# Two adaptive modulations computed with their output columns on the partitions

## The chip, the cores and the metric

The kernel runs on one core of one Trainium2 chip. The metric is the device time of one execution in microseconds. A profile shows one execution: its span, and what TensorE (PE, with its weight loads PEld), VectorE (DVE), ScalarE (ACT), GpSimd (POOL) and SyncE (SP) did in it. Everything is computed in fp32, so TensorE runs two passes for each matmul of the program, and the profile counts both.

## What is computed

Two transformer blocks work one behind the other on x, 512 positions of width 1024. Each starts with a modulation vector of 6 x 1024 numbers, from a condition vector c of its own:

```
mod = silu(c) @ ada_w + ada_b              # c: 1024, ada_w: 1024 x 6144
shift1, scale1, gate1, shift2, scale2, gate2 = split(mod, 6)
h = rmsnorm(x, norm1_w) * (1 + scale1) + shift1
proj = h @ w_in
...                                        # block 1: causal convolution of 4 taps over q, k and v, gated delta
                                           # rule, sparse attention; block 2: pooling and convolution branches
x = x + gate1 * (mixed @ w_out)
h2 = rmsnorm(x, norm2_w) * (1 + scale2) + shift2
...                                        # block 1: feed-forward of width 2816; block 2: retrieved experts
```

## The kernel before

**Layout.** Activations lie with the channels on the 128 partitions: `xT` and `hT` hold 8 channel tiles of 512 positions. The modulation is wanted in the same form: `mod[p, blk, t]` is output 128 t + p of block `blk`, so 48 columns per block, and `eff` is (1 + scale) * norm weight.

**The ada products before.** `ada_w` (25 MB per block) streams on POOL's queue through a ring of four slots, 48 transfers of 512 KB per block, the next into a slot once VectorE has used it (`ada_used`, `ada_2_used`). Inputs lie on the partitions. `matvec` multiplies a tile of 128 inputs x 512 outputs by 128 values of silu(c), one per partition, and adds the next seven tiles to it: 12 groups `g` per block, each one tensor_scalar and seven scalar_tensor_tensor of 512 elements. The sum over the 128 partitions is then made by TensorE: `columns` takes 128 x 128 of the result as weights and a column of ones as the moving operand, which leaves four columns of `mod` in PSUM. `modulation` adds the bias.

**Order of the first block.** The order of each engine is written out by hand; semaphores tie them. VectorE does groups 0 to 2, the first norm, group 3, `modulation(0, 0, 16)`, groups 4 to 7, then `gate_logits`, and with each of the 12 convolutions `conv(m)` half a group of 8 to 11. SP loads param, x and const, and after 8 slots of ada the row weights, the first four w_in tiles and mats. TensorE makes the norm's sum, four groups of columns, the row projection (64 matmuls of 276 columns, result `PS[:, c]`), then 24 w_in blocks `m` of 512 columns, with columns behind blocks 2, 3, 5, 7 and 9, a one-row sum of squares (`many_sum`) behind blocks 2 to 9, the gate's sums behind 3 and the heads' norms (`spread`) from block 11 on, which wait for VectorE's reciprocal (`inverse_many`, behind conv 10). ScalarE applies `eff` and shift to all 8 tiles of `hT`, exponentials of the gate, and Silu and Square of each convolution's result. `conv(m)` on VectorE is one product from PSUM and three multiply-adds (the four taps).

**Second block.** Its ada stream starts after the attention. VectorE does 44 of the 96 half-slot steps beside the 11 double steps of the feed-forward's "up" loop and 52 beside the 8 "down" blocks. TensorE's columns stand behind the first down block (groups 0 to 3), behind the sum of norm 2 (4 to 7) and behind the 28 projections of the second block (8 to 11), ahead of `branches`, which wait for VectorE's layer norm (`yc_ready`). From some 1040 us on, experts are gathered row by row, and `row_dot` (line 2267) multiplies each with the activation and reduces in one tensor_tensor_reduce over 1024 elements, the form that the change uses.

Of the kernel before, what the change touches and what calls it, by code (L numbers as in the profile page):

```python
# [18 lines left out]
P = 128  # L19
S = 512  # L20
# [29 lines left out]
def _cols(widths):  # L50
    out, at = {}, 0
    for name, w in widths:
# [5 lines left out]
    ("ident", P), ("ones", P), ("upper", P), ("strict", P), ("causal", P), ("levels", LEVELS * P),  # L58
    ("cmpneg", NC * NCMP), ("cmpmask", NC * NCMP), ("poolcnt", 4 * 16), ("iota", 16), ("strip", 2 * MANY - 1), ("hscale", 1), ("eps", 1), ("one", 1)])
PARAM, NPARAM = _cols([  # L60
    ("c", KT), ("c_2", KT), ("ada_b", 48), ("ada_b_2", 48), ("norm1", KT), ("norm2", KT), ("norm1_2", KT),
# [6 lines left out]
          ("down", 16, WIDE)]  # L68
FIRST = {}
# [103 lines left out]
def build(nc, a, out):  # L173
    ctx = ExitStack()
    with ctx:
# [15 lines left out]
        silc = sb("silc", [P, 2, KT])  # L191
# [26 lines left out]
        acc = area(19008, 12, S)  # L218
        ring_a = area(26944, SLOTS, 2 * S)
# [52 lines left out]
        acc_2 = area(FT * S + 3072, 12, S)  # L272
        ring_2 = area(FT * S + 9216, SLOTS, 2 * S)
# [140 lines left out]
        modcol_done = sem("modcol_done")  # L414
# [65 lines left out]

        def evicted(t):
# [70 lines left out]
        def _(pe):  # L552
# [32 lines left out]
            def columns(src, blk, g):  # L585

                for q in range(4):
                    ins = mm(PS[:, 6, 48 * blk + 4 * g + q:48 * blk + 4 * g + q + 1], src[:, g, q * P:(q + 1) * P], ones[:, 0:1])
                ins.then_inc(modcol_done, 1)

            pe.wait_ge(inputs_loaded, 32)
            norm(0)

            for g in range(4):
                pe.wait_ge(ada_used, SLOTS * (g + 1))
                columns(acc, 0, g)
            pe.wait_ge(rows_loaded, 16)

            for c in range(NC):
                for k in range(KT):  # L600
                    if c == 0:
                        pe.wait_ge(h_ready, k + 1)
# [41 lines left out]
            def turn(i):  # L644

                if i == 0:
                    pe.wait_ge(mod_ready, 2)
                elif i == 1:
                    pe.wait_ge(hm_normed, 8)
                else:  # L650
                    pe.wait_ge(kv_done, i - 1)
# [6 lines left out]
            for m in range(24):  # L658
# [10 lines left out]
                if m == 2:  # L669
                    for g in range(4, 8):  # L670
                        pe.wait_ge(ada_used, SLOTS * (g + 1))
                        columns(acc, 0, g)
                if m in (3, 5, 7, 9):
                    g = 8 + (m - 3) // 2
                    pe.wait_ge(ada_used, SLOTS * (g + 1))
                    columns(acc, 0, g)
# [128 lines left out]
            pe.wait_ge(rest_loaded, 16)  # L805
# [55 lines left out]
            for m in range(KT):  # L861
                if m == 1:

                    pe.wait_ge(ada_2_used, 4 * SLOTS)
                    for g in range(4):
                        columns(acc_2, 1, g)
# [10 lines left out]
            pe.wait_ge(ada_2_used, 8 * SLOTS)  # L877
            pe.wait_ge(mod_ready, 3)
            for g in range(4, 8):
                columns(acc_2, 1, g)  # L880
# [171 lines left out]
            pe.wait_ge(ada_2_used, 12 * SLOTS)  # L1052
            for g in range(8, 12):
                columns(acc_2, 1, g)
# [82 lines left out]
        def _(act):  # L1137
# [5 lines left out]
            A(silc[:, 0, :], par("c", 0, KT), ACT.Silu).then_inc(silu_c_ready, 1)  # L1143
            act.wait_ge(silu_c_ready, n(silu_c_ready))
            A(silc[:, 1, :], par("c_2", 0, KT), ACT.Silu).then_inc(silu_c_ready, 1)
            act.wait_ge(silu_c_ready, n(silu_c_ready))
            def norm(z, col, shift, final=None, base=0, w=S, parts=None, done=0):
# [14 lines left out]
                for q, part in enumerate([hT] if parts is None else parts):  # L1162
                    for k in range(KT):
                        act.wait_ge(normed, KT * (done + q) + k + 1)
# [30 lines left out]

            for m in range(12):
                act.wait_ge(conv_ready, m + 1)
# [87 lines left out]
            for t in range(NC * NH):  # L1285
# [296 lines left out]
        def _(dve):  # L1582
# [30 lines left out]
            def modulation(blk, lo, hi):  # L1613

                dve.wait_ge(modcol_done, 12 * blk + hi // 4)
                tt(mod[:, blk, lo:hi], PS[:, 6, 48 * blk + lo:48 * blk + hi], par("ada_b" if blk == 0 else "ada_b_2", lo, hi - lo), ADD).then_inc(vec_step, 1)
# [6 lines left out]
            def matvec(blk, g, weights, landed, used, dst, k0=0, k1=KT):  # L1623

                for k in range(k0, k1):
                    j, u = divmod(k, 2)
                    if u == 0:

                        dve.wait_ge(landed[j], g * 16 + 16)
# [923 lines left out]
```

## Time and profile before

| | |
|---|---|
| Median of 3 runs | 2565.99 us (2560.9 to 2567.07) |
| Profiled execution | 2566.99 us, span 2565.3 |
| TensorE matmul / weight load busy | 2293.6 / 1491.4 us |
| VectorE busy | 1719.5 us |
| ScalarE busy | 695.7 us |
| GpSimd busy | 618.9 us |
| HBM read | 745.35 MB |

Busy time is an average over stages with different limits, and a share of it says little of a stage. The granted clock is that of TensorE, 1.00 for 2.4 GHz and 0.50 for 1.2. A line in the kernel can be that of a helper: all matmuls but a few are L554, VectorE's scalar_tensor_tensor are L1593, its tensor_scalar L1590, its tensor_tensor L1587.

### The profile page before, as it was taken

What the parts mean: (1) busy time and instruction counts of PE and PEld (TensorE: products, weight loads), DVE (VectorE), ACT (ScalarE), POOL (GpSimd) and SP (SyncE); (2) the same over time, 40 slices, a digit from 0 to 9 for tenths busy, and PEclk for the clock granted to TensorE, in tenths of its full rate; (3) what the DMA queues carried; (4) which work ended last, traced back from release to release, by engine and by line L of the source; (5) the groups of instructions that cost most, each with busy time, mean ns of one, the idle gap of its engine ahead of it and who ended that gap; (6) DMA issues with size and microseconds to landing.
All of it is one profiled execution on the core that took longest, in us unless ns stands there. A gap on an engine that the chain in (4) does not pass through costs nothing.

```text
span 2565.3 us, 25633 instructions
## 1 busy us (share of the span) xinstructions
PE 2293.6 (89%) x8418; PEld 1491.4 (58%) x8418; DVE 1719.5 (67%) x3782; ACT 695.7 (27%) x1990; POOL 618.9 (24%) x612
## 2 busy tenths in 40 slices
PE   3999998899999998899999998999998877777776
PEld 2544685748888887677777565675444433232222
DVE  6753564617655853778887799877667666676664
ACT  2221122413101111221222322424333333333332
POOL 2100000000001000222332333434444434344342
PEclk7999997899999999999999999999999999999999
DMA  8621102025666433999999999999999999999997
GB/s 304 228 80 57 33 1 66 1 98 197 237 219 240 148 128 124 388 343 369 409 374 390 392 380 371 376 410 409 419 419 419 420 420 420 418 418 420 419 418 295
DMA packets 130584, 748.97 MB, mean 292 GB/s; under 512 B 14497, under 2 KB 14497, under 8 KB 64673
## 3 DMA queue, kind: packets, MB, share of 16 engines
q0 software_dynamic: 87552, 587.24, 57.4%
q1 hardware_dynamic: 42912, 160.26, 17.6%
q8 instruction: 60, 0.98, 0.2%
q14 instruction: 60, 0.48, 0.1%
HBM read 745.35 MB, written 2.10 MB: 291 GB/s over the span
## 4 chain that ended last, share of the span: by engine, by line
PE 62%; DMA 23%; DVE 9%; ACT 4%; issue 2%; another core or an unknown queue 0%; POOL 0%; DVEq 0%; ACTq 0%; POOLq 0%
PE PS L554 61%; DMA arena<-experts_dram,ecur 21%; DVE arena L2267 3%; DVE h_all L1593 2%; DMA arena<-ada_dram 1%; DVE arena L1593 1%; ACT arena L1471 1%; DVE arena L1587 1%; ACT L1467 1%; DVE h_all L1587 1%; ACT const L1478 0%; ACT const L1476 0%; DMA ring<-up_dram 0%; DMA ring<-down_dram 0%; ACT arena L1467 0%
## 5 line engine op out<-in xcount | busy, mean ns | idle before, releaser
L554 PE MATMUL PS<-arena,const 128*128 128x512 f32 (+2 forms) x1872 | 879.5, 614 | 179.6 <-ACT const L1478 165.6
L554 PE MATMUL PS<-h_all,ring 128*128 128x256 f32 (+2 forms) x3584 | 884.2, 405 | 10.5 <-ACT h_all L1166 4.0
L2426 POOL DMA_INDIRECT arena<-experts_dram,ecur x512 | 567.8, 1109 | 1162.7 <-PE PS L554 758.8
L2267 DVE CUSTOM_DVE_ANT_0 arena<-arena 128x1024 f32<-128x1024 f32 x512 | 626.0, 1223 | 293.5 <-DMA arena<-experts_dram,ecur 289.3
L554 PEld LDWEIGHTS PS<-h_all,ring 128*128 128x128 f32 x3584 | 681.8, 191 | 221.7 <-issue 135.6
L554 PEld LDWEIGHTS PS<-arena,const 128*128 128x128 f32 (+1 forms) x1872 | 353.6, 195 | 626.2 <-issue 361.4
L1467 ACT ACTIVATE arena<-arena 128x2 f32<-128x2 f32 x255 | 51.8, 203 | 846.9 <-DVE arena L2267 846.5
L554 PE MATMUL PS<-arena,ring 128*128 128x256 f32 (+1 forms) x960 | 245.3, 417 | 3.7 <-DVE arena L1587 2.6
L554 PEld LDWEIGHTS PS<-arena,ring 128*128 128x128 f32 x960 | 186.8, 195 | 63.9 <-issue 36.6
L554 PE MATMUL PS<-arena 128*128 128x128 f32 (+2 forms) x1088 | 157.1, 305 | 8.6 <-DVE arena L1587 3.5
L554 PEld LDWEIGHTS PS<-arena 128*128 128x128 f32 (+1 forms) x1088 | 143.4, 208 | 28.2 <-issue 8.4
L1593 DVE SCALAR_TENSOR_TENSOR arena<-arena,silc 128x512 f32<-128x512 f32 x168 | 126.3, 752 | 18.0 <-DMA arena<-ada_dram 12.3
L1471 ACT ACTIVATE arena<-arena 128x1 f32<-128x1 f32 x510 | 122.3, 287 | 8.4
L1593 DVE SCALAR_TENSOR_TENSOR xT<-PS,mod,xT 128x256 f32<-128x256 f32 (+1 forms) x56 | 29.0, 520 | 128.3 <-PE PS L554 128.2
L2408 POOL DMA_DIRECT2D arena<-ada_dram x4 | 2.1, 528 | 384.6 <-ACT arena L1294 384.6
L1587 DVE TENSOR_TENSOR arena<-arena 128x256 f32<-128x256 f32 (+9 forms) x185 | 86.4, 467 | 5.4 <-ACT arena L1212 2.7
L2413 POOL DMA_DIRECT2D arena<-ada_dram x44 | 23.2, 528 | 266.3 <-DVE arena L1593 266.3
L1478 ACT ACTIVATE const<-const,arena 128x128 f32<-128x128 f32 x199 | 76.8, 386 | 0.0
L1476 ACT ACTIVATE const<-const,arena 128x128 f32<-128x128 f32 x199 | 76.8, 386 | 0.0
L1593 DVE SCALAR_TENSOR_TENSOR arena<-arena 128x1024 f32<-128x1024 f32 (+3 forms) x93 | 75.8, 815 | 0.6 <-ACT arena L1471 0.3
L1590 DVE TENSOR_SCALAR arena<-PS,param 128x256 f32<-128x256 f32 (+1 forms) x56 | 32.9, 588 | 58.8 <-PE PS L554 57.8
L1593 DVE SCALAR_TENSOR_TENSOR arena<-PS,param,arena 128x255 f32<-128x255 f32 (+3 forms) x124 | 69.4, 559 | 4.4
(246 smaller groups left out, 1591.0 us busy)
## 6 DMA issues: line engine op xcount, KB each, us to landing
arena<-ada_dram POOLq DMA_DIRECT2D x96, 512.0 KB, 5.2
ring<-up_dram SPq DMA_DIRECT2D x88, 512.0 KB, 3.5
ring<-w_in_dram SPq DMA_DIRECT2D x80, 512.0 KB, 3.6
ring<-query_dram SPq DMA_DIRECT2D x32, 512.0 KB
ring<-w_out_dram SPq DMA_DIRECT2D x24, 512.0 KB, 4.0
ring<-down_dram SPq DMA_DIRECT2D x16, 704.0 KB, 4.9
ring<-branch_dram SPq DMA_DIRECT2D x16, 512.0 KB
arena<-experts_dram,ecur POOLq DMA_INDIRECT x512
```

The lines of the kernel that those rows point to most:

```text
L554: return nc.tensor.matmul(o, l, r, start=start, stop=stop)
L1467: A(wts[:, b, :], dots[:, b, :], ACT.Gelu_apprx_tanh).then_inc(gelu_ready, 1)
L1471: A(wts[:, b, k:k + 1], wts[:, b, k:k + 1], ACT.Copy, scale=gcur[:, r % 3, j:j + 1]).then_inc(w_ready2, 1)
L1476: A(diag[:, b, 0, :], ident, ACT.Copy, scale=wts[:, b, 0:1]).then_inc(act_step, 1)
L1478: A(diag[:, b, 1, :], ident, ACT.Copy, scale=wts[:, b, 1:2]).then_inc(diag_ready, 1)
L1587: return V.tensor_tensor(out=o, in0=x, in1=y, op=op)
L1590: return V.tensor_scalar(o, x, s1, s2, op0, op1)
L1593: return V.scalar_tensor_tensor(out=o, in0=x, scalar=s_, in1=y, op0=op0, op1=op1)
L2267: V.tensor_tensor_reduce(out=u, in0=u, in1=hrow[:, (r // HEADS) % 2, :], scale=1.0, scalar=0.0, op0=MUL, op1=ADD, accum_out=dots[:, p % NB ...
L2408: pool.dma_start(ring_2[:, j, :], a["ada_2"][j]).then_inc(slot_2_ready[j], 16)
L2413: pool.dma_start(ring_2[:, j, :], a["ada_2"][bass.ds(i * SLOTS + j, 1)].rearrange("o p n -> p (o n)")).then_inc(slot_2_ready[j], 16)
L2426: nc.gpsimd.indirect_dma_start(out=ring_e[:, g % RING, :], out_offset=None, in_=a["experts"], in_offset=bass.IndirectOffsetOnAxis(ap=ecur[ ...
```

## The change

Both weights are laid out transposed, so that a slot holds 128 outputs on the partitions and all 1024 inputs along them; silu(c) is a row of 1024 that lies on all partitions (`crow`, `crow_2`, 0.5 MB each, loaded as such). One tensor_tensor_reduce then multiplies slot and row and leaves the sum in one column of `mod`. The `columns` on TensorE are gone. The first 16 columns of block 1 get buffers of their own, filled by eight transfers of 1 MB at the start; the other 32, and all of block 2, go through rings of four slots as before. SP's order is new: c's row, two tables of const, x, param, row weights; after 12 columns the w_in tiles, the rest of const and mats. Tiles 4 to 7 of `hT` are modulated by VectorE, 0 to 3 by ScalarE. The product of each convolution's first tap moves from VectorE to ScalarE (`first_tap`).

```diff
+HEAD = 16
-        acc = area(19008, 12, S)
-        ring_a = area(26944, SLOTS, 2 * S)
+        crow = area(23104, D)
+        ring_a = area(26944, SLOTS, D)
+        ada_head = [area(at, 2, D) for at in (0, 2048, 4096, 6144, 8192, 10240, 16960, 19008)]
...
         def _(sp):
-            sp.dma_start(param[:], a["param"]).then_inc(params_loaded, 16)
+            sp.dma_start(crow, a["crow"][0]).then_inc(params_loaded, 16)
+            sp.dma_start(const[:, 0:HEAD_CONST], a["const"][:, 0:HEAD_CONST]).then_inc(inputs_loaded, 16)
             sp.dma_start(xT[:], a["x"]).then_inc(inputs_loaded, 16)
-            sp.dma_start(const[:], a["const"]).then_inc(inputs_loaded, 16)
-            sp.wait_ge(ada_used, 2 * SLOTS)
+            sp.dma_start(param[:], a["param"]).then_inc(rows_loaded, 16)
             sp.dma_start(roww, a["roww"]).then_inc(rows_loaded, 16)
+            sp.wait_ge(ada_used, HEAD - 4)
             for j in range(SLOTS):
                 sp.dma_start(ring[:, j, :D], a["w_in"][j]).then_inc(slot_ready[j], 16)
+            sp.dma_start(const[:, HEAD_CONST:], a["const"][:, HEAD_CONST:]).then_inc(rest_loaded, 16)
             sp.dma_start(mats[:], a["mats"]).then_inc(rest_loaded, 16)
...
# TensorE: behind the row projection
+            pe.wait_ge(rest_loaded, 32)
# TensorE: behind w_in block 2, one of the eight places
-                if m == 2:
-                    for g in range(4, 8):
-                        pe.wait_ge(ada_used, SLOTS * (g + 1))
-                        columns(acc, 0, g)
...
# ScalarE
+            A(crow, crow, ACT.Silu).then_inc(silu_c_ready, 1)
...
+                    for k in range(4):
+                        act.wait_ge(normed, k + 1)
+                        h = hT[:, k, :]
+                        A(h, h, ACT.Identity, bias=shift(k), scale=eff[:, col, k:k + 1]).then_inc(h_ready, 2)
...
+            def first_tap(m):
+                act.wait_ge(blocks_done, m + 1)
+                A(cv[:, m % 2, :], PS[:, m % SLOTS, :], ACT.Copy, scale=par("gconv", 4 * m + 3)).then_inc(qkv_ready, 1)
+            first_tap(0)
             for m in range(12):
+                if m < 11:
+                    first_tap(m + 1)
                 act.wait_ge(conv_ready, m + 1)
                 A(qkv[:, m, :], cv[:, m % 2, :], ACT.Silu).then_inc(qkv_ready, 1)
...
# ScalarE, behind the attention
+            act.wait_ge(crow_2_loaded, 16)
+            A(crow_2, crow_2, ACT.Silu).then_inc(silu_c_ready, 1)
...
# VectorE
+            def ada_column(blk, t):
+                row, used = (crow_2, ada_2_used) if blk else (crow, ada_used)
...
+                V.tensor_tensor_reduce(out=w, in0=w, in1=row, scale=1.0, scalar=0.0, op0=MUL, op1=ADD,
+                                       accum_out=mod[:, blk, t:t + 1]).then_inc(used, 1)
...
-            for g in range(3):
-                matvec(0, g, ring_a, slot_a_ready, ada_used, acc[:, g, :])
+            for t in range(8):
+                ada_column(0, t)
             dve.wait_ge(inputs_loaded, 32)
             norm(0)
-            matvec(0, 3, ring_a, slot_a_ready, ada_used, acc[:, 3, :])
+            for t in range(8, HEAD):
+                ada_column(0, t)
             modulation(0, 0, 16)
+            for k in range(4, KT):
+                ts(hT[:, k, :], hT[:, k, :], eff[:, 0, k:k + 1], mod[:, 0, k:k + 1], MUL, ADD).then_inc(normed, 1)
...
-            for g in range(4, 8):
-                matvec(0, g, ring_a, slot_a_ready, ada_used, acc[:, g, :])
+            for t in range(HEAD, 32):
+                ada_column(0, t)
+            dve.wait_ge(rest_loaded, 32)
             gate_logits()
             for m in range(12):
                 conv(m)
-                if m < 8:
-                    g = 8 + m // 2
-                    matvec(0, g, ring_a, slot_a_ready, ada_used, acc[:, g, :], 4 * (m % 2), 4 * (m % 2) + 4)
+                for t in range(32 + 4 * m // 3, 32 + 4 * (m + 1) // 3):
+                    ada_column(0, t)
...
+            dve.wait_ge(silu_c_ready, 2)
             for i in range(FT // 2):
-                ada_steps(4 * i, 4 * i + 4)
+                ada_steps(2 * i, 2 * i + 2)
...
             for m in range(KT):
-                ada_steps(44 + 13 * m // 2, 44 + 13 * (m + 1) // 2)
+                ada_steps(22 + 13 * m // 4, 22 + 13 * (m + 1) // 4)
...
         def _(pool):
-            for t in range(12 * SLOTS):
-                if t >= SLOTS:
+            for u in range(HEAD // 2):
+                pool.dma_start(ada_head[u], a["ada"][2 * u:2 * u + 2].rearrange("t p n -> p t n")).then_inc(ada_head_ready(u), 16)
+            pool.wait_ge(ada_used, 2 * SLOTS)
+            for t in range(HEAD, 48):
+                j = (t - HEAD) % SLOTS
+                if t >= HEAD + SLOTS:
                     pool.wait_ge(ada_used, t - SLOTS + 1)
-                pool.dma_start(ring_a[:, t % SLOTS, :], a["ada"][t]).then_inc(slot_a_ready[t % SLOTS], 16)
+                pool.dma_start(ring_a[:, j, :], a["ada"][t]).then_inc(slot_a_ready[j], 16)
             pool.wait_ge(att_ready, NC * NH)
+            pool.dma_start(crow_2, a["crow"][1]).then_inc(crow_2_loaded, 16)
```

## Rows read from the trace of the kernel before

**Rows 1.** Chain of waits over the first 200 us (start us, length us, what)

```profile
37.01 3.36 DVE rs L1642
...
55.65 17.74 PE PS L554 x64
...
74.13 126.30 PE PS L554 x345
```

**Rows 2.** Timeline of all engines, 0 to 110 us (start, length, engine, line)

```profile
13.43 1.28 ACT L1149 ACT_TABLE_LOAD   x1 [9.04 <-DMA const<-const_dram]
...
25.24 0.69 ACT L1159 ACTIVATE rs<-PS,const 128x512 f32<-128x512 f32 x1 [1.28 <-PE PS L554]
...
40.40 5.78 DVE L1587 TENSOR_TENSOR h_all<-xT,rs 128x512 f32<-128x512 f32 x8
...
54.69 6.74 ACT L1166 ACTIVATE h_all<-h_all,mod,eff 128x512 f32<-128x512 f32 x8 [28.76 <-DVE eff L1593]
```

**Rows 3.** Timeline of TensorE, 70 to 260 us

```profile
94.83 3.69 PE L554 MATMUL PS<-const,arena 128*128 128x1 f32 x32
98.45 1.89 PE L554 MATMUL PS<-sq,const 128*14 128x512 f32 x2
100.27 7.82 PE L554 MATMUL PS<-h_all,ring 128*128 128x512 f32 x16
...
125.22 0.95 PE L554 MATMUL PS<-const,arena 128*128 128x1 f32 x8
126.09 1.03 PE L554 MATMUL PS<-sq,const 128*14 128x512 f32 x2
127.06 7.13 PE L554 MATMUL PS<-h_all,ring 128*128 128x512 f32 x16
...
174.66 1.12 PE L554 MATMUL PS<-rs,const 14*128 14x512 f32 x2
```

**Rows 4.** Timeline of TensorE, 505 to 1060 us

```profile
747.39 4.24 PE L554 MATMUL PS<-const,arena 128*128 128x1 f32 x32
751.48 69.46 PE L554 MATMUL PS<-arena,ring 128*128 128x256 f32 x308
...
932.00 4.51 PE L554 MATMUL PS<-const,arena 128*128 128x1 f32 x32
```

**Rows 5.** Busy time by stretch (the engines, TensorE clock, DMA share, GB/s)

```profile
4.00:8.00 4.00, 0.00 (x0) 0.00 (x0) 0.00 (x0) 0.35 (x2) 0.00 (x0) 1.00 1.00 421
62.00:70.00 8.00, 8.00 (x36) 6.51 (x36) 5.87 (x9) 1.39 (x5) 2.38 (x5) 1.00 0.90 313
110.00:130.00 20.00, 20.00 (x52) 8.62 (x52) 14.94 (x23) 3.92 (x7) 2.11 (x4) 1.00 0.54 176
```

**Rows 6.** Instructions of line 2267: duration ns, smallest, median, largest

```profile
L2267 DVE CUSTOM_DVE_ANT_0 arena<-arena x512: 1200/1225/1290, 1038.4 to 2553.3; 128x1024 f32<-128x1024 f32 x171
```

**Rows 7.** DMA issues of the first 60 us: count, size, median us to landing

```profile
arena<-ada_dram POOLq DMA_DIRECT2D x23, 512.0 KB, 5.2
xT<-x_dram SPq DMA_DIRECT2D x1, 2048.0 KB, 8.4
```

**Rows 8.** Busy time by stretch, TensorE alone: busy (instructions), granted clock, DMA

```profile
936.00:940.00 4.00, 4.00 (x12) 0.50 0.02 4
580.00:584.00 4.00, 4.00 (x12) 0.63 0.00 0
```

**Rows 9.** Timeline of VectorE, two stretches

```profile
171.09 3.34 DVE L1720 RECIPROCAL rs<-rs 14x512 f32<-14x512 f32 x1
...
934.73 1.43 DVE L1593 SCALAR_TENSOR_TENSOR arena<-sq,arena 128x256 f32<-128x256 f32 x4
```

**Rows 10.** Timeline of all engines behind norm 2

```profile
826.35 5.03 ACT L1166 ACTIVATE h_all<-h_all,mod,eff 128x256 f32<-128x256 f32 x8 [2.43 <-DVE h_all L1587]
...
828.01 6.16 PE L554 MATMUL PS<-h_all,ring 128*128 128x256 f32 x18
```

**Rows 11.** Transfers from ada_dram after 250 us

```profile
DMA to landing us min/median/max: 3.7/5.1/9.5
```

More of the change, by code:

```diff
@@ L479, in build, with ada_head_ready @@
         row_landed = [sem(f"expert_row{j}_ready") for j in range(RING)]
+        def ada_head_ready(u):
+            return (slot_a_ready if u < SLOTS else slot_2_ready)[u % SLOTS]
         def evicted(t):
@@ L644, in turn @@
             def turn(i):
-                if i == 0:
-                    pe.wait_ge(mod_ready, 2)
-                elif i == 1:
+                if i == 1:
                     pe.wait_ge(hm_normed, 8)
-                else:
+                elif i > 1:
                     pe.wait_ge(kv_done, i - 1)
@@ L861, in _ @@
             for m in range(KT):
[L862 to L866, printed above, removed]
                 if m >= 4:
@@ L1161, in norm @@
                 act.wait_ge(mod_ready, min(z + 1, 3))
-                for q, part in enumerate([hT] if parts is None else parts):
+                if z == 0:
+                    for k in range(4):
+                        act.wait_ge(normed, k + 1)
+                        h = hT[:, k, :]
+                        A(h, h, ACT.Identity, bias=shift(k), scale=eff[:, col, k:k + 1]).then_inc(h_ready, 2)
+                        n(h_ready)
+                        n(h_ready)
+                    act.wait_ge(h_ready, KT)
+                    return
+                for q, part in enumerate(parts):
                     for k in range(KT):
-                        act.wait_ge(normed, KT * (done + q) + k + 1)
+                        act.wait_ge(normed, KT // 2 + KT * (done + q) + k + 1)
                         h = part[:, k, :]
@@ L1613, in modulation @@
             def modulation(blk, lo, hi):
-                dve.wait_ge(modcol_done, 12 * blk + hi // 4)
-                tt(mod[:, blk, lo:hi], PS[:, 6, 48 * blk + lo:48 * blk + hi], par("ada_b" if blk == 0 else "ada_b_2", lo, hi - lo), ADD).then_inc(vec_step, 1)
+                used = ada_2_used if blk else ada_used
+                dve.wait_ge(used, n.now(used))
+                if blk == 0 and lo == 0:
+                    dve.wait_ge(rows_loaded, 32)
+                tt(mod[:, blk, lo:hi], mod[:, blk, lo:hi], par("ada_b" if blk == 0 else "ada_b_2", lo, hi - lo), ADD).then_inc(vec_step, 1)
                 dve.wait_ge(vec_step, n(vec_step))
@@ L1621, in modulation @@
                         dve.wait_ge(mod_ready, n(mod_ready))
[L1623 to L1629, printed above, removed]
-                    w = weights[:, j, u * S:(u + 1) * S]
-                    c_ = silc[:, blk, k:k + 1]
-                    if k == 0:
-                        ts(dst, w, c_, None, MUL, ALU.bypass).then_inc(vec_step, 1)
-                    else:
-                        stt(dst, w, c_, dst, MUL, ADD).then_inc(used if u else vec_step, 1)
-                    dve.wait_ge(used if u else vec_step, n(used if u else vec_step))
+            def ada_column(blk, t):
+                row, used = (crow_2, ada_2_used) if blk else (crow, ada_used)
+                if blk:
+                    dve.wait_ge(slot_2_ready[t % SLOTS], 16 * (t // SLOTS) + 32)
+                    w = ring_2[:, t % SLOTS, :]
+                elif t < HEAD:
+                    dve.wait_ge(ada_head_ready(t // 2), 16)
+                    w = ada_head[t // 2][:, t % 2, :]
+                else:
+                    i = t - HEAD
+                    dve.wait_ge(slot_a_ready[i % SLOTS], 16 * (i // SLOTS) + 32)
+                    w = ring_a[:, i % SLOTS, :]
+                V.tensor_tensor_reduce(out=w, in0=w, in1=row, scale=1.0, scalar=0.0, op0=MUL, op1=ADD,
+                                       accum_out=mod[:, blk, t:t + 1]).then_inc(used, 1)
+                n(used)
             def norm(t, parts=((hT, 0, S, 0),)):
```

64 lines of the change are left out of this document (21 added, 43 removed).

## The prediction

> **What bounds the kernel now.** I read the chain of waits over the first 200 us first. It shows a head in which the work waits on VectorE and on the transfers of the ada weights: VectorE's reciprocal stands on the chain at 37.01, the first projection runs at 55.65, and the w_in blocks begin at 74.13 and then follow one another on TensorE with no other engine between [rows 1]. The timeline of all engines fills in that head: ScalarE turns to x at 13.43, the norm's root ends at 25.24 + 0.69 = 25.93, VectorE normalises until 46.18, and the first modulated tile is made at 54.69 [rows 2]. Third, the timeline of TensorE alone: from 74 to 250 us, and again from 736 to 967, its matmuls touch, so what is taken out there is time; one-column matmuls ("128x1") stand at five places of the first stretch and three of the second [rows 3, 4]. Busy times by stretch confirm it: in 110 to 130 us TensorE is busy 20.00 of 20.00 us and VectorE 14.94 [rows 5]. The expert part behind it is not touched and hangs on what comes before; I let it move as a block.
>
> My sum is made against the profiled execution, 2566.99 us (span 2565.3), 1.0 above the median of the three timed runs, 2565.99.
>
> **Head.** Before, the 16 columns that the first modulation needs cost VectorE four groups of one product and seven multiply-adds, waits included. After, they are 16 multiply-and-reduce instructions over 128x1024. That very instruction stands 512 times in the expert part: 1225 ns, with an accumulator read of 83 ns that overlaps its end; I take 1.23 us for each [rows 6]. The row's ends, 1200 and 1290, make 0.5 us less or 1.0 more over 16.
> Their weights now come in eight transfers of 1 MB, all issued at once on POOL's queue, while SP's queue has the row of c (0.5 MB), a little of const, x (2.1 MB), param and roww (1.5 MB). When do they land? The 16 engines move 0.42 MB per us with both queues full [rows 5]. x landed 8.4 us after its issue, at about 9.7, while the ada slots issued beside it came later, so the software queue had the smaller share beside x [rows 7]. I take x at 11.5 us (0.3 MB more ahead of it), SP's five transfers done at about 17 with 1.9 MB of ada, and from there a pair of columns each 2.5 us: the fourth pair at 21.9. VectorE then ends column 8 at 24.4. The root comes 12.5 us after x (13.43 to 25.93 before [rows 2]): 24.0. So the norm starts at 24.4; its reciprocal and eight products take 9.2 (37.01 to 46.18 [rows 1, 2]): 33.6. Columns 9 to 16, all landed by 33, take 8 x 1.23 = 9.8: 43.4; bias and eff 0.5: ScalarE starts at 43.9 instead of 54.69, 10.8 gained.
> Half of the tiles are now modulated on VectorE. TensorE took 17.74 us for the 64 matmuls, the first eight tiles paced by ScalarE at 6.74/8 = 0.84 us each [rows 1, 2]; at half clock it needs nearly that itself, so I take 0.5 gained (0 to 2). Together 11.3: w_in begins at 62.8. SP's w_in tiles now wait for column 12 at 38.5 and bring const's rest and mats with them, 3.4 MB, 8 us at that rate: landed at 47, 15 us before TensorE asks. POOL's issues wait for column 8 and hold up nothing else.
>
> **The w_in blocks.** Gone are 32 one-column matmuls at 94.83, which hold the next one back by 3.62 us; behind them the sum takes 1.89 us instead of 1.03 and the block 7.82 instead of 7.13, the clock having fallen: 1.55 more. Gone are four groups of eight, 0.87 each from start to start (125.22 to 126.09), 3.5 [rows 3]. Sum 8.6.
> The granted clock behind the last group of such matmuls is 0.50, the lower level of 1.2 GHz, in 936 to 940, although TensorE is busy 4.00 of 4.00 us [rows 8]. The Trainium skill ("TensorE: Matmul & The Clock Gate", What's actually happening) says that the clock is throttled by default and that activity releases it. Taken plainly, one-column matmuls are activity and their removal would give no clock back: 23.2 us gained in all instead of 27.7. The trace doesn't agree, and I go by the row.
> New waits in this stage. VectorE's columns 17 to 32 come between the norm and conv 0, 2 us after it (four tiles modulated). Four lie ready; the others cycle through four slots, a landing of 5.2 us [rows 7] and 1.5 of use and issue, so 1.7 per column: 45.9 + 4.9 + 20 = 71. Then the gate's exponentials with table loads (3.3), ScalarE's new first tap (0.6), conv, Silu and Square: the first sum of squares can run at about 80 and is wanted at 62.8 + 20.7 = 83.5 [rows 3]. Hidden, with 3.5 us to spare. Later VectorE has less per block (three taps of 0.75 and 4/3 columns, 3.9 us, against TensorE's 8.0), and first taps on ScalarE, busy 3.92 of 20 us [rows 5], cost nothing. One place has no slack: the reciprocal of the head norms ended at 171.09 + 3.34 = 174.43, and TensorE's spread ran at 174.66 [rows 3, 9]. Now a column of 1.23 us stands ahead of it on VectorE: TensorE waits 1.0. Net of the stage: 7.6.
>
> **The "up" loop** is TensorE's; two columns (2.5 us) replace four half-row steps (2.9) beside it: nothing. c's second row lands and passes Silu under the w_out blocks: nothing; without that cover, a landing and a table load, some 6 us.
>
> **The "down" blocks.** The 32 matmuls at 747.39 push the next by 4.09 us, and the 308 after them take 69.46 us, where 7 blocks at the settled 9.5 need 66.5: 3.0 of clock [rows 4]. Both go: 7.05.
>
> **Behind norm 2** the columns lie under the norm. ScalarE starts its first tile at 826.35, ready at 827.0; TensorE comes at 828.01 [rows 10]. It gains 1.0, but is then paced by ScalarE: 0 to 1.5, I take 1.0.
>
> **Before the branches** the columns run from 932.00 for 4.51 us [rows 4], but the branches need VectorE's last product, which ends at 934.73 + 1.43 = 936.16 [rows 9]. This group is replaced by an idle wait: 0.2 gained of 4.4. The clock afterwards: 0.50 behind columns, 0.63 behind a pure pause of 4 us [rows 8]; I take 0.5 back (0 to 2.5). Together 0.7.
>
> Sum: 11.3 + 7.6 + 7.05 + 1.0 + 0.7 = 27.7. 2566.99 - 27.7 = 2539.3, told as **2539**.
>
> **Rivals.**
> A, even shares: x and the ada pairs have half of the engines each. For: the pairs stand in line from the start. Against: x was ahead of its half before [rows 7]. Then x lands when 5.5 MB have moved, at 15.2, root at 27.7, the norm 3.3 later than forecast: 2542.6. The Trainium skill ("DMA: Bandwidth & Descriptors", Queues, rings and completion order) has such a rule, engines that take turns between queues packet by packet; x's row doesn't bear out equal bytes.
> B, the clock isn't given back, since short sums and gate matmuls stand at the same places: 1.55 + 3.0 are lost again, 2543.8. Against: long blocks back to back on both sides.
> C, a new wait behind the ring: each landing takes its worst value, 9.5 us [rows 11]. Then 11 us per four columns, VectorE ends column 32 at 84 instead of 71, the first sum comes at 93, TensorE waits 9.7 us and resumes at low clock (1.5): 2550.5. It decides once a column costs more than 2.0 us. For: four slots, each of shorter use than before. Against: the median 5.2.
> D, slower: the 8.4 MB on POOL's queue run ahead of x, at a poor rate. At 313 GB/s, which 0.90 busy engines moved while the ada stream was almost alone [rows 5], x lands at 37.6 and ScalarE starts 25.7 later than forecast: 2565. It decides against the change from x at 39.6 us on, where the 27.7 are used up; at 250 GB/s, an estimate somewhat below the row, x lands at 46.6: 2574, which I give as its time. Against: x's 8.4 us.
>
> **Numbers.** Forecast 0.63, A 0.15, B 0.10, C 0.07, D 0.05. A measurement can tell 0.3%, 7.7 us, from no change. Forecast, A, B and C are faster by more: 0.95. D is split: same 0.03, slower 0.02. Range: downward the first tiles' 1.5, norm 2's 0.5, the clock's 2 and, as runs before lay up to 5 below their median, some of that: 2532. Upward A and B inside, C in part: 2548.
>
> **What would show it.** In the profile after: ScalarE's first h_all tile near 44; 96 more of the custom instruction at 1225 ns; w_in's first block near 63; no 128x1 matmul, and behind the third block a sum of 1.03, not 1.89; a TensorE pause of 1 us behind the twelfth block, of 3.7 us behind norm 2's sum and of 4 us ahead of the branches; from 1040 on the same work 27 us earlier. Wrong would be: x past 15 us, columns 17 to 32 at over 2 us each, or a granted clock of 0.5 in the second down block.

## The result and the profile after

The median of the changed kernel's four runs is 2532.78 us, that of the kernel before beside it on the same chip 2563.44 us (2558.43 to 2567.07). One of the four took 6322.47 us for a reason that the record doesn't show; it is in that median and in nothing else here, and the other three lie between 2527.9 and 2533.1. The ratio is 0.9875, 95% interval [0.986, 0.989]: 32 us gained, worked out as 0.0125 x 2563.44. The forecast was 2539 with a range of 2532 to 2548: the median lies 0.8 us inside its fast end, the ratio times the kernel before (2531.4) 0.6 us outside. The profiled execution took 2532.46 us, its span 2530.8 us against 2565.3 before: 34.5 us, where the sum of the prediction had 27.7.

First the head, from the timeline of all engines of the changed kernel (start, length, engine, line, what; in brackets the idle time before it and what ended it). Its rows answer to [rows 1, 2].

```profile
12.53 1.27 ACT L1133 ACTIVATE sq<-xT 128x512 f32<-128x512 f32 x2
...
14.68 1.23 DVE L1636 CUSTOM_DVE_ANT_0 arena<-arena 128x1024 f32<-128x1024 f32 x1 [14.68 <-DMA arena<-ada_dram]
...
19.71 1.23 DVE L1636 CUSTOM_DVE_ANT_0 arena<-arena 128x1024 f32<-128x1024 f32 x1 [2.65 <-DMA arena<-ada_dram]
...
22.72 0.69 ACT L1136 ACTIVATE rs<-PS,const 128x512 f32<-128x512 f32 x1 [1.28 <-PE PS L562]
...
24.82 1.22 DVE L1636 CUSTOM_DVE_ANT_0 arena<-arena 128x1024 f32<-128x1024 f32 x1 [0.17 <-DMA arena<-ada_dram]
...
27.12 3.35 DVE L1644 RECIPROCAL rs<-rs 128x512 f32<-128x512 f32 x1
30.50 5.77 DVE L1584 TENSOR_TENSOR h_all<-xT,rs 128x512 f32<-128x512 f32 x8
36.31 1.23 DVE L1636 CUSTOM_DVE_ANT_0 arena<-arena 128x1024 f32<-128x1024 f32 x1
...
46.15 2.93 ACT L1143 ACTIVATE h_all<-h_all,mod,eff 128x512 f32<-128x512 f32 x4 [22.75 <-DVE eff L1590]
47.11 16.93 PE L562 MATMUL PS<-arena,h_all 128*128 128x276 f32 x64 [24.49 <-ACT h_all L1143]
64.83 10.54 PE L562 MATMUL PS<-h_all,ring 128*128 128x512 f32 x24 [0.80 <-issue]
```

The reader is to see that the root of the sum of squares ends at 23.41, while VectorE, waiting for pairs of weights at 14.68, 19.71, 22.27 and 24.82, can begin the reciprocal only at 27.12. The chain of waits of the same execution names what it hung on (start, length, what):

```profile
3.74 21.06 DMA arena<-ada_dram
```

TensorE alone, the timeline that answers to [rows 3, 4]:

```profile
85.60 1.03 PE L562 MATMUL PS<-sq,const 128*14 128x512 f32 x2
86.56 7.13 PE L562 MATMUL PS<-h_all,ring 128*128 128x512 f32 x16
...
158.03 1.12 PE L562 MATMUL PS<-rs,const 14*128 14x512 f32 x2 [0.94 <-DVE rs L1723]
159.08 8.83 PE L562 MATMUL PS<-h_all,ring 128*128 128x512 f32 x16
167.84 1.12 PE L562 MATMUL PS<-rs,const 14*128 14x512 f32 x2
...
373.41 1.12 PE L562 MATMUL PS<-arena,const 14*128 14x512 f32 x2
374.46 2.94 PE L562 MATMUL PS<-arena 128*128 128x128 f32 x24
377.33 1.98 PE L562 MATMUL PS<-arena,const 14*128 14x512 f32 x4
...
491.62 2.81 PE L562 MATMUL PS<-arena,ring 128*128 128x512 f32 x6 [0.56 <-ACT arena L1289]
...
711.68 77.93 PE L562 MATMUL PS<-arena,ring 128*128 128x256 f32 x352 [2.20 <-DVE arena L1584]
791.24 0.70 PE L562 MATMUL PS<-rs,const 128*128 128x256 f32 x2 [1.64 <-DVE rs L1584]
795.69 37.74 PE L562 MATMUL PS<-h_all,ring 128*128 128x256 f32 x160 [3.75 <-ACT h_all L1152]
...
905.02 30.78 PE L562 MATMUL PS<-arena,ring 128*128 128x256 f32 x128 [4.26 <-DVE arena L1590]
```

No 128x1 matmul is left. The sum behind the third block takes 1.03 us and its next block 7.13, where before they took 1.89 and 7.82 [rows 3]; the down blocks run in one piece; a wait of 0.94 stands at 158.03 and one of 4.26 at 905.02, both as forecast, and one of 3.75 at 795.69, behind norm 2's sum, where 3.7 was forecast.

The following table gives the lengths between the same points of both programs: the first w_in block, the first spread of a head norm (14x512), the second, the first w_out block, the first up block, the first down block, norm 2's sum, the first block behind it, the first branch block, the block behind the branches, and the end.

| stretch | touched | before | after | gained | forecast |
|---|---|---|---|---|---|
| start to w_in | yes | 74.13 | 64.83 | 9.3 | 11.3 |
| w_in to first spread | yes | 100.53 | 93.20 | 7.3 | 7.6 |
| first to second spread | no | 8.11 | 9.81 | -1.7 | 0 |
| second spread to w_out (attention) | no | 334.29 | 323.78 | 10.5 | 0 |
| w_out to up | no | 62.70 | 63.66 | -1.0 | 0 |
| up | no | 156.34 | 156.40 | -0.1 | 0 |
| down, to norm 2's sum | yes | 86.55 | 79.56 | 7.0 | 7.05 |
| sum to first block | yes | 5.36 | 4.45 | 0.9 | 1.0 |
| to the first branch block | yes | 108.41 | 109.33 | -0.9 | 0.2 |
| branches | no | 31.82 | 32.31 | -0.5 | 0.5 |
| to the end | no | 1597.06 | 1593.47 | 3.6 | 0 |

The sum is 34.5 (with roundings). The head and the four other touched stretches gave 23.6 of the 27.15 forecast for them; the untouched ones, where the forecast had 0.5, gave 10.9. So the missing gain and the surplus are two questions, and the surplus is the larger.

### The profile page after: what moved, and what is told of

Same layout as the page of the kernel before. It is cut to its first block, busy times and chain, and to the rows that moved or that the text cites. A ratio compares the mean times of both kernels' runs of the same rounds, so it can differ in the third digit from the quotient of the medians.

```text
span 2530.8 us, 25155 instructions
## 1 busy us (share of the span) xinstructions
PE 2255.1 (89%) x8226; PEld 1456.7 (58%) x8226; DVE 1687.2 (67%) x3774; ACT 702.0 (28%) x1999; POOL 611.9 (24%) x605
## 4 chain that ended last, share of the span: by engine, by line
PE 60%; DMA 23%; DVE 11%; ACT 4%; issue 2%; POOL 0%; another core or an unknown queue 0%; DVEq 0%; ACTq 0%; POOLq 0%
PE PS L562 59%; DMA arena<-experts_dram,ecur 21%; DVE arena L2270 4%; DVE h_all L1590 2%; DVE arena L1584 1%; DMA arena<-ada_dram 1%; ACT arena L1468 1%; ACT L1464 1%; DVE arena L1590 1%; DVE h_all L1584 1%; ACT const L1475 0%; DVE arena L1636 0%; ACT const L1473 0%; DMA ring<-down_dram 0%; DMA ring<-w_out_dram 0%
## 5 line engine op out<-in xcount | busy, mean ns | idle before, releaser
L2270 DVE CUSTOM_DVE_ANT_0 arena<-arena 128x1024 f32<-128x1024 f32 x512 | 625.9, 1222 | 291.6 <-DMA arena<-experts_dram,ecur 288.2
L562 PE MATMUL PS<-arena 128*128 128x128 f32 (+2 forms) x1088 | 149.3, 296 | 9.3 <-DVE arena L1584 3.5
L562 PEld LDWEIGHTS PS<-arena 128*128 128x128 f32 (+1 forms) x1088 | 136.3, 199 | 27.4 <-DVE arena L1584 7.0
L1636 DVE CUSTOM_DVE_ANT_0 arena<-arena 128x1024 f32<-128x1024 f32 x96 | 114.1, 1223 | 26.5 <-DMA arena<-ada_dram 25.2
L1590 DVE SCALAR_TENSOR_TENSOR xT<-PS,mod,xT 128x256 f32<-128x256 f32 (+1 forms) x56 | 29.1, 520 | 129.9 <-PE PS L562 129.6
```

Source lines behind the costliest of these rows:

```text
L562: return nc.tensor.matmul(o, l, r, start=start, stop=stop)
L1590: return V.scalar_tensor_tensor(out=o, in0=x, scalar=s_, in1=y, op0=op0, op1=op1)
L1636: V.tensor_tensor_reduce(out=w, in0=w, in1=row, scale=1.0, scalar=0.0, op0=MUL, op1=ADD, accum_out=mod[:, blk, t:t + 1]).then_inc(used, 1)
L2270: V.tensor_tensor_reduce(out=u, in0=u, in1=hrow[:, (r // HEADS) % 2, :], scale=1.0, scalar=0.0, op0=MUL, op1=ADD, accum_out=dots[:, p % NB ...
```

## Experiments

Twelve runs followed, on three chips, each beside runs of the kernel before on its own chip.

**The changed kernel again, and the kernel before again.** No edit. What was on record for the first:

> The changed kernel once more. The first pair of traces shows 14.9 us gained at the fourteenth w_in block and 25.4 at the end of the attention, although nothing between them was changed; TensorE's granted clock was 0.50 for 24 us less there. Theory 1 (luck): how long the clock stays low in the unchanged attention differs from execution to execution of one kernel; then this profile's stretch from block 13 to the end of the attention is longer than 316 us (the kernel before had 326), and the ratio comes out nearer 0.992 (21 us gained). Theory 2 (systematic): the stretch is again about 316 us and the ratio again 0.9875 (32 us).

and for the second:

> The kernel before once more, for its profile. Theory 1: the stretch from block 13 to the end of the attention varies by several us around 326 and may reach 316. Theory 2: it is again 326 within 1.

Measured: 2533.6 us (2530.28 to 2538.7) against 2565.63, ratio 0.9883 [0.9865, 0.9902]; the kernel before profiled at 2562.51. In the repeated profile of the changed kernel the attention stretch runs from 166.08 to 499.05: 332.97 us, not 323.78. TensorE's timeline shows where. These rows are the same instructions as the after rows 373.41 to 377.33 above:

```profile
373.20 2.07 PE L562 MATMUL PS<-arena,const 14*128 14x512 f32 x2
375.20 4.70 PE L562 MATMUL PS<-arena 128*128 128x128 f32 x24
379.82 1.98 PE L562 MATMUL PS<-arena,const 14*128 14x512 f32 x4
...
499.05 2.38 PE L562 MATMUL PS<-arena,ring 128*128 128x512 f32 x5 [0.56 <-ACT arena L1289]
```

Busy times by stretch show the clock beside it (bounds, length, then busy us of TensorE, weight loads, VectorE, ScalarE, GpSimd, the granted clock, DMA share, GB/s), first of the changed kernel's first profile, then of this one:

```profile
369.00:373.00 4.00, 3.04 (x20) 2.02 (x19) 3.16 (x5) 0.60 (x1) 0.00 (x0) 1.00 0.01 4
373.00:377.00 4.00, 4.00 (x29) 3.12 (x28) 2.09 (x3) 0.39 (x1) 0.00 (x0) 1.00 0.00 0
```

```profile
368.00:372.00 4.00, 3.05 (x19) 2.03 (x18) 3.44 (x5) 0.60 (x1) 0.00 (x0) 1.00 0.01 4
372.00:376.00 4.00, 4.00 (x12) 2.27 (x12) 2.13 (x3) 0.00 (x0) 0.00 (x0) 0.51 0.00 0
```

In the 4 us ahead TensorE was as busy in both (3.04 and 3.05 of 4.00 us), with the same waits; in one the granted clock stays at 1.00, in the other it falls to 0.51 in the mean of 4 us (0.50 is the 1.2 GHz level), and 24 matmuls take 4.70 us instead of 2.94. One and the same kernel thus has this stretch in two lengths, 9.2 us apart. What follows: the 10.5 us of the first pair of profiles are no property of the change alone.

The two theories on record were each met in one half. From block 13 to the end of the attention the repeated profile took 324.9 us, not 316 again: the first. But the ratio is 0.9883 and its interval leaves out the 0.992 of the first theory, so the timed gain of 30 us stands as in the first measurement. The kernel before, repeated, has 334.46 us in its attention, as the second theory said. This second pair of profiles is 26.1 us apart, 21.6 from the touched stretches and 4.5 from the others, where the first pair had 34.5 = 23.6 + 10.9: the forecast of 27.7 lies between the two.

**The one-column matmuls put back**, on constant data, at their eight places (they leave the columns to VectorE and only cost TensorE time):

```
+            def idle_columns(groups):
...
+                for q in range(4 * groups):
+                    mm(PS[:, 6, q:q + 1], ident, ones[:, 0:1])
...
+                if m == 2:
+                    idle_columns(4)
+                if m in (3, 5, 7, 9):
+                    idle_columns(1)
```

and idle_columns(4) behind the second down block, behind norm 2's sum and ahead of the branches.

> The change, but with the one-column matmuls put back on TensorE at their eight old places, on other data (their results are used by nobody). My terms: 3.6 us and 1.55 of clock behind block 2, 3.5 at four places, 4.1 and 3.0 of clock behind the first down block, nothing behind norm 2 and before the branches, where they fill a wait: 15.7 us more than the changed kernel. If the clock falls there for another reason, 11.2. If those under the waits cost too: up to 24.

Measured: 2549.04 us (2543.93 to 2553.41), 0.9941 [0.9921, 0.9962], 15.4 above the changed kernel of the same chip, where 15.7 was expected. The parts fit less well than the sum, which is partly luck. By stretch against the changed kernel: w_in to spread 103.17 against 93.20 (+10.0, expected 8.65), down 84.83 against 79.56 (+5.3, expected 7.1), norm 2's sum to block 6.02 against 4.45 (+1.6, expected 0), to the branches 109.37 against 109.33, branches 32.30 against 32.31. TensorE's timeline:

```profile
86.26 4.34 PE L562 MATMUL PS<-const 128*128 128x1 f32 x32
90.53 1.89 PE L562 MATMUL PS<-sq,const 128*14 128x512 f32 x2
92.34 8.83 PE L562 MATMUL PS<-h_all,ring 128*128 128x512 f32 x16
101.01 0.95 PE L562 MATMUL PS<-const 128*128 128x1 f32 x8
...
722.52 11.45 PE L562 MATMUL PS<-arena,ring 128*128 128x256 f32 x44 [2.21 <-DVE arena L1597]
733.81 3.63 PE L562 MATMUL PS<-const 128*128 128x1 f32 x32
737.30 68.41 PE L562 MATMUL PS<-arena,ring 128*128 128x256 f32 x308
```

Behind the columns the clock is lost here: its windows show a granted clock of 0.50 from 90 to 94 us, with TensorE busy 4.00 of 4.00. (The Trainium skill's rule in "TensorE: Matmul & The Clock Gate", What's actually happening, that activity releases the clock, would have made these matmuls free of that price; this run disagrees, with 0.50.) But it isn't lost each time. The kernel before in its third profile, TensorE's timeline:

```profile
93.66 3.63 PE L554 MATMUL PS<-const,arena 128*128 128x1 f32 x32
97.22 1.03 PE L554 MATMUL PS<-sq,const 128*14 128x512 f32 x2
98.18 7.13 PE L554 MATMUL PS<-h_all,ring 128*128 128x512 f32 x16
```

The same 32 columns stand there, and the sum and the block behind them run as if there were none; its second profile has the same lengths. In the down blocks all profiles with columns lose some: the 308 matmuls behind them take 68.15 to 69.46 us, where 66.5 is the settled rate. Rival B, that the clock isn't given back once the columns are gone, falls by the eight profiles of kernels without them: the third block's sum takes 1.03 us and the next block 7.13, and the down blocks 77.93, in each. Removing the columns is worth about half of the whole gain. The 32 ahead of the branches cost nothing, since VectorE's product is waited for there anyway.

**The head norms' reciprocal ahead of its column**, for the wait of 0.94:

```
+                if m == 10:
+                    inverse_many(1, rs[0:MANY, 0, :])
                 for t in range(32 + 4 * m // 3, 32 + 4 * (m + 1) // 3):
                     ada_column(0, t)
...
-                if m == 10:
-                    inverse_many(1, rs[0:MANY, 0, :])
```

> The change, with the reciprocal of the head norms ahead of the ada column behind conv 10. In the changed kernel TensorE waits 0.94 us there, and the next block takes 8.83 us instead of 7.13 since the clock falls. Theory: both go, 2.6 us gained. Rival: ScalarE's root, now made behind the first tap of block 11, is what the reciprocal waits for; then the wait shrinks but stays and the clock may fall anyway: 0 to 1 us.

Measured: 2530.92 us (2527.72 to 2532.69), 0.9871 [0.9852, 0.989], 2.7 below the unchanged copy beside it, within both intervals. In its profile the wait is gone (w_in to spread 92.27, 0.93 less) and the second spread comes 8.11 us behind the first. But the repeated changed kernel also has 8.11 there, with its wait of 0.94; the 1.7 us of a slower block after the wait are lost in some executions only (in three of the six profiles that have the wait, in none of the three without it). The edit is worth 0.9 us in its stretch, and 2.6, as expected, only where the clock falls too; the timed runs can't tell it from nothing.

**Bulk transfers behind the ones first needed.** SP issues param and roww (1.4 MB) once VectorE is through column 5:

```
             sp.dma_start(xT[:], a["x"]).then_inc(inputs_loaded, 16)
+            sp.wait_ge(ada_used, 5)
             sp.dma_start(param[:], a["param"]).then_inc(rows_loaded, 16)
```

> The change, but SP's param and row weights (1.5 MB) are issued behind the fifth ada column instead of at once. In the changed kernel the pairs of columns 3 to 8 landed at 19.7, 22.3 and 24.8 us, 2.7 later than I had taken, and the head was 2.2 longer. Theory (the engines are shared by bytes): without the 1.5 MB they land 3 us sooner, the norm starts at 23.8 instead of 27.1, and w_in 3.3 sooner. Rival (the software queue gives a 1 MB pair each 2.6 us whatever lies beside it): the same times as now, 0.

Measured: 2526.58 us (2525.97 to 2532.33), 0.9852 [0.9836, 0.9869]. The timeline of VectorE and of TensorE shows the pairs ready earlier (fourth at 21.69, not 24.82) and the first w_in block at 61.86, 3.0 us ahead of 64.83 (3.3 expected). On the same chip two kernels with the unchanged head, profiled below, have that block at 66.46 and 66.77, so the edit is worth 3 to 5 us there:

```profile
14.12 1.22 DVE L1637 CUSTOM_DVE_ANT_0 arena<-arena 128x1024 f32<-128x1024 f32 x1 [14.12 <-DMA arena<-ada_dram]
...
21.69 1.23 DVE L1637 CUSTOM_DVE_ANT_0 arena<-arena 128x1024 f32<-128x1024 f32 x1 [0.19 <-DMA arena<-ada_dram]
...
61.86 20.84 PE L563 MATMUL PS<-h_all,ring 128*128 128x512 f32 x48 [0.80 <-issue]
```

That is the head's missing 2 us and one more: the weights were late because 1.4 MB that nothing needed yet went beside them. The DMA issues of the first 45 us (count, size, median us to landing) show the same from the other side, first in the changed kernel, then with the late bulk:

```profile
xT<-x_dram SPq DMA_DIRECT2D x1, 2048.0 KB, 10.6
...
arena<-roww_dram SPq DMA_DIRECT2D x1, 1104.0 KB, 15.8
```

```profile
xT<-x_dram SPq DMA_DIRECT2D x1, 2048.0 KB, 10.9
arena<-roww_dram SPq DMA_DIRECT2D x1, 1104.0 KB, 9.9
```

x did not gain from it. The timed ratios, 0.9852 and 0.9873 for the kernel with the taps back, have intervals that overlap; the profiles carry this reading.

**Three edits together:** the two above, and the first eight columns as transfers of 512 KB instead of pairs:

```
-            for u in range(HEAD // 2):
+            for t in range(8):
+                pool.dma_start(ada_head[t // 2][:, t % 2, :], a["ada"][t]).then_inc(ada_head_ready(t)[0], 16)
+            for u in range(4, HEAD // 2):
...
```

> The change with three edits: reciprocal ahead of the column, param and row weights late, and the first eight columns in transfers of 512 KB instead of 1 MB. Theory: 2.6 of which half is clock, 3.3, and 1.1 (the last column that the norm waits for is used one column sooner): 6 us under the changed kernel, some 2526. Rival: VectorE is then bound by its own work from the root on: 4.

Measured: 2527.02 us (2525.77 to 2530.07), 0.9852 [0.9836, 0.9868]: no better than the late bulk alone. The timeline of VectorE says why: columns start 2.4 us earlier and are through by 21.8, at 24.0 with the late bulk alone, and then VectorE waits for ScalarE's root. The head's bound has moved from the weights to x and its sum of squares; the first w_in block stands at 62.77.

```profile
11.71 1.23 DVE L1639 CUSTOM_DVE_ANT_0 arena<-arena 128x1024 f32<-128x1024 f32 x1 [11.71 <-DMA arena<-ada_dram]
...
24.26 3.35 DVE L1647 RECIPROCAL rs<-rs 128x512 f32<-128x512 f32 x1 [2.49 <-ACT rs L1139]
```

**First taps back on VectorE**, one part of the change undone:

```
+                if m >= 2:
+                    dve.wait_ge(qkv_ready, m - 1)
...
-                dve.wait_ge(qkv_ready, 2 * m if m else 1)
+                ts(o, y, par("gconv", 4 * m + 3), None, MUL, ALU.bypass).then_inc(vec_step, 1)
+                dve.wait_ge(vec_step, n(vec_step))
```

(and first_tap taken off ScalarE).

> The change without one part: each convolution's first tap is VectorE's again. Theory: VectorE has 3.9 us per block against 8.0 of TensorE, so 0, within 0.5 us in the stretch of the w_in blocks. Rival: the taps on ScalarE are part of the gain: up to 12 x 0.7 = 8 us slower.

Measured: 2534.68 us (2530.87 to 2534.92), 0.9873 [0.9856, 0.9889]; w_in to spread 93.16 against 93.20. The part is worth nothing in its stretch, as costed.

**128 unused bytes ahead of the large buffer** in the changed kernel, one profile only:

```
+        gap = sb("gap", [P, 32])
```

> The changed kernel with 128 unused bytes in SBUF ahead of the arena, so that the buffers of the gathered rows lie where they lay in the kernel before (the change made param and silc 128 bytes smaller). The expert part is 4 us shorter in all four profiles of the changed family than in both of before: rows 256 to 320 of a tile 168.2 to 168.4 against 169.7 to 170.0. Theory (place in SBUF): 170 again, 4 us more in all. Rival (place in HBM, or the DMA stream itself): 168.

Measured: 2540.4 us, span 2538.7; attention 332.97 us again, as in the repeated changed kernel. On the question asked: the last 256 gathers took 652.1 us from first start to last start, where the eight other profiles of the changed family have 649.5 to 650.2 and the three of the kernel before 653.0 to 654.0. By this one profile the place in SBUF would account for about two thirds of that difference, and neither theory is met whole.

**The same in the kernel before**, with gaps of 384 and of 464 bytes, to see whether its untouched stretches move with nothing of the change in them:

```
+        gap = sb("gap", [P, 96])        # the second kernel: 116
```

> The kernel before with 384 unused bytes ahead of the arena, which puts the gathered rows 512 bytes on from where the changed kernel has them. With 128 bytes of gap the changed kernel's last 256 gathers took 652.1 us instead of 649.2 to 650.1; before had 653.0 and 653.3. Theory (alignment in SBUF, by 512 bytes or a divisor of it): about 650 here, 3 us less than before. Rival (absolute place, or something else in the change): 653. In the unchanged attention stretch: luck of the clock's phase lets it come out at about 324 or 333 in this family too (before: 334 twice); a systematic effect of the change lets it be 334 again.

> The kernel before with 464 unused bytes ahead of the arena, so that it starts at a multiple of 512 bytes, counted from the first buffer. Theory: last 256 gathers at 650 or under. Rival: 653.

> The kernel before a third time, for the attention stretch from block 13 to its end: 334.3 and 334.5 in the two profiles so far, while the changed family had 323.8 four times, 331.5 twice and 333.0 twice. Luck: any of these values. Systematic: 334.

Measured: 2557.32 us (2548.74 to 2561.56), 0.9991 [0.9976, 1.0006], and 2557.36 (2553.52 to 2560.37), 0.9998 [0.9985, 1.0012]: the same as before, within the interval. But in their profiles the attention stretch took 323.72 and 326.80 us, with 334.42 in the plain kernel before beside them. Their last 256 gathers took 651.2 and 651.1 us, beside 654.0: lower, but not the 650 of the theory. TensorE's timeline with the 384 bytes, the same instructions as in the two quotations above, and the window over them:

```profile
182.82 1.12 PE L555 MATMUL PS<-rs,const 14*128 14x512 f32 x2
...
388.32 1.12 PE L555 MATMUL PS<-arena,const 14*128 14x512 f32 x2
389.37 2.94 PE L555 MATMUL PS<-arena 128*128 128x128 f32 x24
...
506.54 1.96 PE L555 MATMUL PS<-arena,ring 128*128 128x512 f32 x4 [0.56 <-ACT arena L1295]
```

```profile
387.00:395.00 8.00, 7.34 (x40) 4.96 (x40) 4.78 (x10) 1.75 (x3) 0.00 (x0) 1.00 0.01 2
```

The kernel before, with nothing of the change in it but 384 unused bytes more, has the short attention stretch too.

**The version to keep:** late bulk, early reciprocal, and a gap of 80 bytes that puts the large buffer on a multiple of 512 bytes.

> The change with the reciprocal ahead of the column, param and row weights late, and the arena at a multiple of 512 bytes. Late alone gave 0.9852 and all three edits 0.9852; there w_in began at 61.9 and 62.8. Theory: 61.9 for w_in, 92.3 to the first spread, 8.1 behind it, gathers at 650: 0.9850, some 2527. If the multiple of 512 makes gathers cheaper still, 2 to 3 us less.

Measured: 2524.07 us (2522.2 to 2526.25) against 2559.55, 0.9868 [0.9847, 0.9889]; span 2522.9. Its first w_in block is at 62.99, w_in to spread 92.27, attention 326.90, the last 256 gathers 649.9: the block is 1.1 us later than expected, and the multiple of 512 bytes made no gather cheaper. The expected ratio of 0.9850 lies at the edge of the interval. Against the late bulk alone the ratios, each to the before of its own chip, don't tell a difference.

## Why the prediction was wrong in its size

Direction held, and so did most of the terms; their sum, 27.7, is 4 us short of the 32 measured, which puts the time at the fast edge of the range. That it is so near is partly luck: the touched stretches gave 3.5 us less than forecast and the untouched ones 10.4 more. Point by point:

**Down blocks, 7.05 forecast: 6.99.** With the columns put back 5.3 of it went again; the clock behind them cost 1.9 us in that profile, 3.0 in the three of the kernel before.

**The w_in stage, 7.6 forecast: 7.3, and then 1.7 lost behind it.** VectorE was through column 32 at 74 us (forecast 71) and the sum at 85.60 waited for nothing; rival C did not occur. The new wait at the reciprocal was 0.94 where I had 1.0. What I had not costed is that the clock can fall behind this wait: the next block took 8.83 instead of 7.13 in the first profile, though not in the second. And the 1.55 of clock behind block 2 that I counted as gained does not belong to each execution either: two other profiles of the kernel before have 98.92 for this stretch, not 100.53. Against those the stretch gained 5.7.

**Head, 11.3 forecast: 9.3.** The root came at 23.41 (24.0 forecast), the norm's first instruction at 27.12 (24.4). The mis-sized term is the landing of the fourth pair, 24.82 against 21.9: x, issued at 1.80, was in use at 12.5, about 1 us later than taken, and roww, which I had done at about 17, landed at 18.5 (15.8 us after its issue at 2.74). Rival A's time for the norm (27.7) was nearly met, though x was not as late as it said (15.2); the late-bulk run shows which of the two it was. Part of the loss came back: eight columns took 9.2 us, not 9.8, since each starts 1.147 us after the one before.

**Behind norm 2, 1.0: 0.9, and taken back.** The first block starts sooner, but the 160 matmuls then take 37.74 us instead of 36.81. The bound I gave, "paced by ScalarE: 0 to 1.5", held its lower end. It is the clock: by windows of 4 us the granted clock is 0.50 from 795 to 799 and 0.66 to 803 in the changed kernel, 0.50 from 827 to 831 and 0.86 to 835 in the kernel before, and 1.00 behind that in both. From the first of the 160 matmuls on, (1 - clock) x time is then 3.0 us against 2.1, an estimate that accounts for the 0.9.

**Before the branches, 0.7: nothing.** TensorE idles 4.26 us where it had issued columns, as forecast, but the 128 matmuls behind it take 30.78 us, 0.5 longer and not 0.5 shorter. Columns put back there changed nothing either.

**The step that failed is "I let it move as a block".** I said it of the expert part and treated attention the same way, as unchanged and therefore worth 0. The lengths from all profiles, in us. "Lost to the clock" is (1 - granted clock) x time, summed over 20 equal windows of the attention stretch; the last column runs from the first to the last of the 512 multiply-and-reduce instructions of the expert part:

| kernel profiled | attention | lost to the clock | expert part |
|---|---|---|---|
| before, three profiles | 334.29, 334.46, 334.42 | 29.1, 28.9, 29.1 | 1514.9, 1512.1, 1515.6 |
| before, 384 and 464 bytes | 323.72, 326.80 | 17.2, 20.4 | 1512.2, 1509.8 |
| changed, two profiles | 323.78, 332.97 | 17.2, 27.3 | 1510.8, 1507.5 |
| columns put back | 323.85 | 17.3 | 1509.6 |
| reciprocal early; taps on VectorE | 331.46, 331.45 | 25.7, 25.5 | 1506.8, 1507.4 |
| late bulk; three edits | 323.84, 323.78 | 17.3, 17.2 | 1508.2, 1508.9 |
| 128 bytes; version to keep | 332.97, 326.90 | 27.3, 20.3 | 1510.0, 1507.6 |

The ends of the expert part are in such rows of VectorE (count, smallest, median, largest ns, first and last start), here of the third profile of the kernel before and of the repeated changed kernel:

```profile
L2267 DVE CUSTOM_DVE_ANT_0 arena<-arena x512: 1203/1225/1285, 1032.7 to 2548.3; 128x1024 f32<-128x1024 f32 x171
```

```profile
L2270 DVE CUSTOM_DVE_ANT_0 arena<-arena x512: 1201/1225/1296, 1015.2 to 2522.7; 128x1024 f32<-128x1024 f32 x171
```

Attention takes 324 to 334 us, and the table says what differs: TensorE idles 25.8 to 26.0 us in it in all fourteen profiles, and length less what the clock took is 305 to 307 us in each. The same changed kernel has both 323.78 and 332.97, and the kernel before with a gap 323.72. No mechanism by which the change shortens it was shown. What stays open is why the plain kernel before lay at 334 three times of three, and what picks the length: buffers were shifted in the short runs of the kernel before, and the stretch began at another time. The timed runs have no trace, but they are wide enough for it: on one chip alone 19 executions of the plain kernel before lie between 2551.8 and 2563.3, five of them at 2555.5 or less, with the next at 2557.9. Whether those five had the short attention isn't shown.

The expert part is 1512 to 1516 us in the plain kernel before and 1507 to 1511 in all changed ones, some 6 us less in the mean (1514.2 against 1508.5); with only a gap the kernel before has 1512.2 and 1509.8. The place of the gather buffers thus can explain about half of it. In the last 256 gathers the families don't overlap, 653.0 to 654.0 against 649.5 to 650.2, and three of the four kernels with a moved buffer lie between (651.1 to 652.1; the version to keep has 649.9), which points the same way. Single profiles don't prove it, and the timed ratios of those kernels, 0.9991 and 0.9998, bound the gain from the gap itself at 0.24% or 6 us. The rest is open.

So of the measured 30 to 32 us, 22 to 24 come from the touched stretches and some 5 from the expert part, by the profiles. The remainder would be which length of attention the timed runs met; that is argued and not shown. The range should have carried the untouched stretches with their own spread of 10 us, not with "some of that".

## What to carry to other kernels

Unchanged code is not worth 0 in a sum but 0 with a spread: where short matmuls between waits go with a falling granted clock, as in this attention stretch, profile the kernel twice and take the difference of that stretch into the range. The one-column matmuls here cost TensorE their own time and, in most profiles, clock behind them; price both, the second as a range, and look for the wait that they hid, since it stays (4.26 us here). A bulk transfer that nothing needs yet delays whatever lands beside it: issue it behind the first need (3.0 us here for one added wait).

## What the hardware showed that I had not expected

The granted clock fell at 372 us in one execution and not in another of the same kernel, TensorE having been equally busy ahead of it; the same stretch then took 332.97 instead of 323.78 us.

Behind the same wait of 0.94 us the next block took 8.83 us in three profiles and 7.13 in three others.

32 one-column matmuls, back to back for 4.34 us, were followed by a granted clock of 0.50 and a block of 8.83 us, with TensorE busy throughout; the 32 of the kernel before, 3.63 us long, were followed by a block of 7.13 in two of its three profiles.

The multiply-and-reduce instruction, shown at 1.22 us, starts every 1.147 us when several follow one another (36.31 to 44.34 for the first and eighth, in seven steps).
